# Attention stage of a hybrid DeltaNet/attention block: shared projection tiles spread over three turns each, evicted in the turn they end in, later gates loaded into the earlier gates' buffers, and the second projection's blocks moved into the last turn

## What is computed

```python
def merge(o_dn, o_na, gt, w_pa, w_pb, w_out):
    g_a, g_b = jnp.split(jax.nn.sigmoid(gt), 2, axis=-1)
    return (g_a * (o_dn @ w_pa) + g_b * (o_na @ w_pb)) @ w_out
...
    s_nb = jnp.where(col_mask[:, :, None, :], s_nb + bias.astype(jnp.float32), -jnp.inf)
    s_ctx = jnp.einsum('bpcqhd,bjhd->bhpcqj', qb, k_ctx, preferred_element_type=jnp.float32)
    m = jnp.maximum(jnp.max(s_nb, axis=(-2, -1)), jnp.max(s_ctx, axis=-1))
    e_nb = jnp.exp(s_nb - m[..., None, None])
    e_ctx = jnp.exp(s_ctx - m[..., None])
    denom = jnp.sum(e_nb, axis=(-2, -1)) + jnp.sum(e_ctx, axis=-1)
```

## Time and profile before

| | us |
|---|---|
| median of 3 runs | 1408.74 |
| lowest, highest | 1407.41, 1413.54 |
| profiled execution, its own time | 1407.62 |
| its span in the profile | 1405.8 |
| mean granted TensorE clock in it | 0.993 |

### The profile page before, as it was taken

The page is one execution under the profiler, slowest core; times in us unless marked ns, Lnnn a source line. Parts: engine busy times, 40 slices in busy tenths (PEclk is TensorE's granted clock), DMA queues, the critical chain, the costliest instruction groups (busy, mean ns, idle before and its releaser), DMA issues.

```text
span 1405.8 us, 26274 instructions
## 1 busy us (share of the span) xinstructions
PE 1358.4 (97%) x10442; PEld 1270.0 (90%) x10442; DVE 814.2 (58%) x1739; ACT 672.3 (48%) x1480; POOL 224.0 (16%) x189
## 2 busy tenths in 40 slices
PE   5999999999999999999999998999999999999998
PEld 4888989899998989999897877999999999999998
DVE  6466655756565565656535654757866434666422
ACT  4463736455373645537346554436655212555321
POOL 1020020202002020200030322000344002444100
PEclk8999999999999999999999999999999999999999
DMA  9552533142333324213426223522232322332332
GB/s 312 201 139 75 153 95 111 55 132 74 89 107 95 111 56 140 66 59 113 130 70 218 68 69 117 169 76 61 60 91 61 103 73 68 103 90 62 83 90 68
DMA packets 202560, 144.49 MB, mean 103 GB/s; under 512 B 8719, under 2 KB 188215, under 8 KB 202183
## 3 DMA queue, kind: packets, MB, share of 16 engines
q1 hardware_dynamic: 202439, 142.82, 34.3%
HBM read 126.77 MB, written 17.99 MB: 103 GB/s over the span
## 4 chain that ended last, share of the span: by engine, by line
PE 75%; DVE 12%; ACT 6%; issue 3%; SPq 2%; DMA 2%; POOL 0%; DVEq 0%; ACTq 0%
PE ps L1199 23%; PE ps L1728 16%; PE ps L1765 11%; PE ps L1498 7%; PE ps L1425 2%; PE ps L1369 1%; DVE tri L2613 1%; PE ps L1432 1%; PE ps L1273 1%; PE ps L1444 1%; DVE tri L2654 1%; DMA W<-in_w_in 1%; DVE W_r L2607 1%; PE ps L1443 1%; PE ps L1375 1%
## 5 line engine op out<-in xcount | busy, mean ns | idle before, releaser
L1199 PE MATMUL ps<-hT_r,WAH_r 128*128 128x320 f32 x912 | 228.4, 331 | 5.6 <-ACT zs L2061 2.4
L1199 PE MATMUL ps<-xT_r,WAH_r 128*128 128x320 f32 x912 | 207.4, 308 | 0.0
L1199 PEld LDWEIGHTS ps<-hT_r,WAH_r 128*128 128x128 f32 x912 | 145.0, 189 | 24.8 <-issue 11.5
L1199 PEld LDWEIGHTS ps<-xT_r,WAH_r 128*128 128x128 f32 x912 | 152.6, 188 | 0.0
L1199 PE MATMUL ps<-hT_r,W_r 128*128 128x320 f32 x592 | 133.9, 309 | 0.0
L1765 PE MATMUL ps<-a_part,W_r 128*128 128x320 f32 x704 | 132.3, 310 | 0.0
L3155 POOL TENSOR_TENSOR gm<-sqkq,dt 128x1280 f32<-128x1280 f32 x8 | 23.5, 2938 | 572.8 <-DVE Xc L2649 502.5
L1765 PEld LDWEIGHTS ps<-a_part,W_r 128*128 128x128 f32 x704 | 110.3, 188 | 0.0
L1728 PE MATMUL ps<-t_big_r,W_r 128*128 128x320 f32 x380 | 107.2, 310 | 0.6 <-ACT naT L2316 0.5
L1728 PE MATMUL ps<-b_part,W_r 128*128 128x320 f32 x456 | 101.4, 309 | 1.4 <-DVE oT_r L2925 1.4
L1199 PEld LDWEIGHTS ps<-hT_r,W_r 128*128 128x128 f32 x592 | 99.1, 189 | 0.0
(11 more groups left out here) (436 smaller groups left out, 3258.9 us busy)
## 6 DMA issues: line engine op xcount, KB each, us to landing
oT<-in_ffn_w SPq DMA_DIRECT2D x44, 512.0 KB, 5.2
W<-in_w_in SPq DMA_DIRECT2D x36, 512.0 KB, 4.0
WAH<-in_w_ada SPq DMA_DIRECT2D x18, 1024.0 KB, 6.8
naT<-in_w_in SPq DMA_DIRECT2D x24, 512.0 KB, 4.2
oT<-in_ffn_w SPq DMA_DIRECT2D x16, 704.0 KB, 4.6
ext_dram<-naT SPq DMA_DIRECT2D x28, 320.0 KB, 4.1
GCB<-gc_dram SPq DMA_DIRECT2D x7, 640.0 KB, 4.2
W<-in_w_pa SPq DMA_DIRECT2D x8, 512.0 KB, 3.7
```

The source lines that it names most:

```text
L1199: m = e.matmul(ps[:, bank + b, 0:n], w[:, k, :], x[:, k, a:a + n], start=k == 0 and i == 0, stop=k == KD - 1 and i == 2, skip_group_check= ...
```

## The change

- `pa_slots`: tile 1 has slots 0 to 7. Tile n from 2 on starts in turn 3n - 4 and has slots 1 and 2 of that turn, and slots 0, 1 and 2 of each of the two turns after it. From turn 2 on no block stands in the fourth slot of a turn, nor in the first slot of a tile's first turn. Tiles end in turns 1, 4, 7, 10, 13, 16 and 19.
- `PA_OUT`: a tile is evicted in VectorE's turn of the same number as TensorE's turn in which it ends, and `pa_evict` stands behind `for_next_pair` in it. `PA_HI` and `PA_LO` move to turns 3n - 6 and 3n - 5, so that `pa_lo_of(n + 1)` stands right behind `pa_evict(n)` in one turn for n from 1 to 6. `pa_evict(0)` moves ahead of three `o_small`.
- `tB` is gone: the later gates are loaded into `tA`. Those of tiles 0 and 1 are loaded when w_pa's tiles 6 and 7 have been evicted, and SP's chain of waits is gone. The loads of w_out's first two tiles now stand behind the eviction of tile 7 in SP's order.
- Blocks (1, 0), (1, 1), (1, 2) and (1, 3) of the second product are placed around block (0, 3), behind `PT` of the last unit instead of the last `out`.
- Waits for the stores of new_k and new_v move from SP to ScalarE and VectorE.

```diff
@@ -195,19 +195,22 @@
 
 def pa_slots():
 
-    return {(n - 1) * (2 * G) // (KD - 1) + k: (n, k) for n in range(1, KD) for k in range(KD)}
+    slots = {k: (1, k) for k in range(KD)}
+    for n in range(2, KD):
+        slots.update({4 * (3 * n - 4) + at: (n, k) for k, at in enumerate((1, 2, 4, 5, 6, 8, 9, 10))})
+    return slots
 
 
 PA_AT = pa_slots()
-PA_LAST = {0: -1, **{n: slot // 4 for slot, (n, k) in PA_AT.items() if k == KD - 1}}
-PA_OUT = {PA_LAST[n] + 1: n for n in range(1, KD)}
-PA_HI = {PA_LAST[n - 2] + 1: n for n in range(2, KD)}
-PA_LO = {PA_LAST[n - 2] + 2: n for n in range(2, KD)}
+PA_LAST = {n: slot // 4 for slot, (n, k) in PA_AT.items() if k == KD - 1}
+PA_OUT = {turn: n for n, turn in PA_LAST.items()}
+PA_HI = {3 * n - 6: n for n in range(2, KD)}
+PA_LO = {3 * n - 5: n for n in range(2, KD)}
 NA_HI = {NT * (p + 1) + 2: p for p in range(KP - 1)}
 NA_LO = {NT * (p + 1) + 4: p for p in range(KP - 1)}
 PB_HI = {PAIRS_OF_HEADS - 3: 0, PAIRS_OF_HEADS - 2: 1}
 PB_LO = {PAIRS_OF_HEADS - 2: 0, PAIRS_OF_HEADS - 1: 1}
-assert len(PA_AT) == KD * (KD - 1) and len(PA_OUT) == len(PA_HI) + 1 == KD - 1
+assert len(PA_AT) == KD * (KD - 1) and len(PA_OUT) == len(PA_HI) + 1 == KD - 1 and max(PA_AT) < 4 * PAIRS_OF_HEADS
 
 PE_FIRST = {1: "sums k", 2: "turn v", 3: "turn c", 4: "turn k"}
 PE_SECOND = {0: "sums q", 1: "sums c"}
@@ -690,7 +693,6 @@
         sb("under_pb", [P, 6 * TOK - 8 * KD], merging)
         pb_big = sb("pb_big", [P, 2, KP, P], merging, F32R)
         ysum = sb("ysum", [P, 2, TOK], merging)
-        tB = sb("tB", [P, 2, TOK], merging)
         yB = sb("yB", [P, 2, TOK], merging)
         merging.close()
 
@@ -965,7 +967,7 @@
                 e.dma_start(tA[:, n % 2, :], ext_dram[NA_N + n, :, :]).then_inc(ld_gate[n % 2], 16)
 
             def tB_in(n):
-                e.dma_start(tB[:, n % 2, :], ext_dram[NA_N + KD + n, :, :]).then_inc(ld_gate[n % 2], 16)
+                e.dma_start(tA[:, n % 2, :], ext_dram[NA_N + KD + n, :, :]).then_inc(ld_gate[n % 2], 16)
 
             def wo_in(n):
                 e.dma_start(wo_slot[n % 4], wo[:, :, n * P:(n + 1) * P]).then_inc(ld_o[n % 4], 16)
@@ -1042,14 +1044,11 @@
                 e.wait_ge(dve_na.sem, dve_na.after(f"k out {p}"))
                 e.dma_start(A["new_k"][0, 0].rearrange("t h d -> t (h d)")[:, p * P:(p + 1) * P], kout[:, :]).then_inc(st_k, 16)
 
-            tile_ended = {turn: n for n, turn in PA_LAST.items() if n and n + 2 < KD}
             for j in range(PAIRS_OF_HEADS):
                 p, i = j // NT, j % NT
-                if j in PA_OUT or not j:
-                    n = PA_OUT[j] if j else 0
-                    if n + 2 < KD:
-                        e.wait_ge(pa_out, n + 1)
-                        tA_in(n + 2)
+                if not j:
+                    e.wait_ge(pa_out, 1)
+                    tA_in(2)
                 if i == NT - 1 and p + 1 < KP:
                     for hh in range(2):
                         e.wait_ge(pool_na, 2 * CT * (p + 1) - 1 + hh)
@@ -1057,9 +1056,16 @@
                 if not i:
                     new_v(p)
                     new_k(p)
-                if j in tile_ended:
-                    e.wait_ge(pa_mm, tile_ended[j])
-                    pa_in(tile_ended[j] + 2)
+                if j in PA_OUT:
+                    n = PA_OUT[j]
+                    if n + 2 < KD:
+                        e.wait_ge(pa_mm, n)
+                        pa_in(n + 2)
+                    e.wait_ge(pa_out, n + 1)
+                    if n + 2 < KD:
+                        tA_in(n + 2)
+                    else:
+                        tB_in(n + 2 - KD)
                 if not i and 1 <= p < KP - 1:
                     e.wait_ge(pe_na.sem, pe_na.after(f"PV {j - 1}"))
                     cv_in(p + 1)
@@ -1068,15 +1074,6 @@
                 wo_in(n)
             e.wait_ge(st_x, 16)
             e.dma_start(xT[:, :, :], x_dram[:, :, :]).then_inc(ld_xT, 16)
-            e.wait_ge(st_k, 16 * KP)
-            e.wait_ge(st_v, 16 * KP)
-            e.wait_ge(st_S, 16 * 2 * H + 32)
-            e.wait_ge(act_na.sem, act_na.after(f"out {PAIRS_OF_HEADS - 1}"))
-            e.wait_ge(dve_na.sem, dve_na.after(f"P {G - 1}"))
-            e.wait_ge(pool_na, 2 * CT * KP)
-            e.wait_ge(pa_out, KD)
-            for n in range(2):
-                tB_in(n)
             for n in range(2, KD):
                 if n + 2 < KD:
                     e.wait_ge(pb_mm, n - 1)
@@ -1654,12 +1651,17 @@
             pb_block(0, 1)
             values(PAIRS_OF_HEADS - 1)
             pb_block(0, 2)
-            wait(act_na, f"out {PAIRS_OF_HEADS - 1}")
-            for n in range(KD):
+            wait(act_na, f"PT {G - 1}")
+            e.wait_ge(pb_lo, 2)
+            pb_block(1, 0)
+            pb_block(1, 1)
+            pb_block(0, KP - 1).then_inc(pb_mm, 1)
+            pb_block(1, 2)
+            pb_block(1, KP - 1).then_inc(pb_mm, 1)
+            for n in range(2, KD):
                 e.wait_ge(pb_lo, n + 1)
-                if n >= 2:
-                    e.wait_ge(y_sum, 2 * n - 3)
-                for k in range(0 if n else KP - 1, KP):
+                e.wait_ge(y_sum, 2 * n - 3)
+                for k in range(KP):
                     m = pb_block(n, k)
                 m.then_inc(pb_mm, 1)
 
@@ -2230,6 +2232,8 @@
             wait(dve_na, f"P {G - 1}")
             wait(pe_na, f"PV {PAIRS_OF_HEADS - 1}")
             e.wait_ge(pool_na, 2 * CT * KP)
+            e.wait_ge(st_k, 16 * KP)
+            e.wait_ge(st_v, 16 * KP)
             for n in range(KD):
                 if n + 2 < KD:
                     pb_hi_of(n + 2)
@@ -2811,12 +2815,11 @@
                 e.wait_ge(wo_hi, n + 1)
                 e.tensor_tensor(wo_small[n % 4], wo_slot[n % 4], wo_big[:, n % 4, :, :], ALU.subtract).then_inc(wo_lo, 1)
 
-            for k in range(KD - 1):
+            for k in range(KD):
                 o_small(k)
                 if k == KD - 4:
                     pa_lo_of(1)
-            pa_evict(0)
-            o_small(KD - 1)
+                    pa_evict(0)
             def minimum(g):
                 p, hh, c = UNITS[g]
                 _, _, (lo, hi) = key_tiles(c)
@@ -2874,9 +2877,9 @@
                     scaled_P(2 * j - 1)
                 else:
                     k_out(0)
+                for_next_pair(DVE_NEXT, j)
                 if j in PA_OUT:
                     pa_evict(PA_OUT[j])
-                for_next_pair(DVE_NEXT, j)
                 if j in PA_LO:
                     pa_lo_of(PA_LO[j])
                 if j in NA_LO:
@@ -2892,12 +2895,14 @@
             e.scalar_tensor_tensor(gain2[:, :, :], mods[:, 32:40, :], 1.0, cols[:, N2:N2 + 8].unsqueeze(2).to_broadcast([P, KD, 2]), ALU.add, ALU.mult).then_inc(mods_done, 1)
             e.tensor_scalar(mods[:, 16:24, :], mods[:, 16:24, :], 0.5, None, ALU.mult).then_inc(mods_done, 1)
             e.wait_ge(mods_done, 3)
+            e.wait_ge(st_v, 16 * KP)
+            e.wait_ge(st_k, 16 * KP)
             for n in range(KD):
                 i = n % 2
                 e.wait_ge(pb_mm, n + 1)
                 e.wait_ge(ld_gate[i], 16 * (KD // 2 + n // 2 + 1))
                 for b, (a, w) in enumerate(HALVES):
-                    m = e.scalar_tensor_tensor(yB[:, i, a:a + w], tB[:, i, a:a + w], 1.0, ps[:, 2 * i + b, 0:w], ALU.add, ALU.mult)
+                    m = e.scalar_tensor_tensor(yB[:, i, a:a + w], tA[:, i, a:a + w], 1.0, ps[:, 2 * i + b, 0:w], ALU.add, ALU.mult)
                 m.then_inc(y_sum, 1)
                 e.wait_ge(y_sum, 2 * n + 1)
                 if n >= 2:
```

## The result

| | before | changed |
|---|---|---|
| median, us | 1409.87 (4 runs) | 1417.26 (4 runs, 1416.61 to 1418.65) |
| profiled execution, us | 1407.62 | 1416.61 |
| its span, us | 1405.8 | 1414.8 |

What follows compares the result with a forecast made beforehand. TensorE, busy 97% of the span, was taken as the bound. Terms -8.0 + 0.5 + 16.0 - 1.95 gave +6.6 us, with +4.8 for the clock +11.4: median 1408.7 to 1420 us, range 1409 to 1425.

Steps and rivals of the forecast that it cites:

- waits that go in the turns: TensorE's waits for `PT`, `hT` and some scores in the turns vanish: 3.9, 3.0 and 1.1 us, 8.0 us saved.
- blocks apart: Pairs of blocks that lay side by side across a turn's border are separated: some 12 cases, 0.5 us lost.
- waits of the scores, turns 1, 4, 7, 10, 13, 16: Scores after tile ends wait for VectorE's eviction, split and two minima: six stalls of 2.1 to 3.2 us.
- another wait of scores, 853 us: In the turns, no second wait was seen behind the forecast stalls: 0 us.
- falls of the clock: Three of six new stalls bring TensorE's clock to half rate: 4.8 us lost; bounds none and 9.6 us.
- last turn, `P 38` and `P 39`: Turn 19: `P 38` stands behind eviction, `naT_r` and w_pb's small part on VectorE: 1.0 us lost.
- tail up to tile 2: Second product: blocks fill the `naT_r` wait, 1.0 us, and shorten tile 2's wait, 0.95 us: 1.95 us saved.
- tail, late loads: Third gate load queues behind xT and w_out on SP, so `yB` of tile 2 may wait: 0 taken, bounds 0 and 1 us.
- the earlier eviction of tile 0 brings nothing: Before scores(1): block (1, 0) starts some 1.4 us earlier, but scores(1) waits for the same VectorE work: 0 us.
- The first rival: In the turns, stalls come but the clock stays up: +6.6 us, 1415.3 us, from 1413 to 1418; chance 0.22.
- Half as long: In the turns, stalls are half as long and cancel the removed waits: -1.4 us, about 1407 us; chance 0.12.
- no stall: In the turns, `-max` is done early with eviction under TensorE's other work: -9.5 us, 1399 us; chance 0.06.

Runs made afterwards that it cites:

- split_first: Changed kernel with the split (small part of w_pa's next tile) ahead of the eviction in VectorE's turn; ratio 1.0014 to the kernel before.
- evict_next: Changed kernel with the eviction back in VectorE's next turn, behind both scaled_P and ahead of for_next_pair; ratio 1.0006 to the kernel before.
- between: Changed kernel with the eviction in VectorE's next turn, between the minima and scaled_P; ratio 0.9969 to the kernel before.
- fill_half: Changed kernel with two fillers (matmuls whose result nobody reads) behind the ends of tiles 1 to 6; ratio 1.0045 to the kernel before.
- between_xt3: between with the xT load cut into eight pieces, two at its old place, one behind each later gate load; ratio 0.9944 to the kernel before.
- xt_pieces3: Changed kernel with the xT load cut into eight pieces, two at its old place, one behind each later gate load; ratio 1.0080 to the kernel before.
- tail_xt: Kernel before with only the change's tail (later gates in tA, tile 1 around block (0, 3)) and xT's load in eight pieces; ratio 0.9984.

## Why the prediction was right, point by point

| step | forecast, us | measured, us |
|---|---|---|
| waits that go in the turns | -8.0 | -8.2 |
| blocks apart | +0.5 | about -0.3, what is left over |
| waits of the scores, turns 1, 4, 7, 10, 13, 16 | 3.2, 2.4, 2.2, 2.1, 2.4, 2.7 | 3.0, 2.3, 2.1, 2.0, 2.3, 2.6 |
| another wait of scores, 853 us | 0 | +0.2 |
| falls of the clock | +4.8 | +2.8 |
| last turn, `P 38` and `P 39` | +1.0 | +1.4 |
| tail up to tile 2 | -1.95 | -2.1 |
| tail, late loads | 0, bounds 0 and 1 | +1.0 |
| sum | +11.4 | +9.0 in the profiles, +7.4 by the medians |

*The stalls.* Each of the six was worked out from rows of before to within 0.2 us. split_first, evict_next and between show that the queue is the cause: the blocks stayed in their new places and the order on VectorE alone moved the turns from 127.9 to 120.9, 119.9 and 114.6 us. This part of the forecast was right by its mechanism.

*The waits that go.* All 13 waits in the turns after 752 us, 8.2 us in all, are gone. I had kept 0.3 us of them. That the earlier eviction of tile 0 brings nothing was right: block (1, 0) starts at 748.2 in place of 749.8, and scores(1) at 751.4 in both.

*The clock* is the term that was mis-sized. I took three falls at 1.6 us; the trace has two, and fill_half prices one at 1.4 us. Three of the six stalls was a choice between bounds, and no row of before could tell it from two or none; that it came near was luck in part. The Trainium skill (TensorE: Matmul & The Clock Gate, "A second HAM failure mode: psum-queue depth-cycling") says that short idles, repeated often enough, make the gate swing. The trace agrees in part: falls stand behind two of the six stalls. The first rival, stalls with the clock up, would have ended 2.8 us lower in the turns. That is all that the traces hold against it: it forecast +6.6 us, which is nearer to the +7.4 us of the medians than my +11.4 us is.

*The tail.* Up to tile 2 the forecast holds: block (0, 2) to tile 2 took 8.6 us and takes 6.4 us. Tile 2 itself waits 0.9 us where I had 0.8. In the last turn I counted the wait of `turn_P(38)` and not that `turn_P(39)` waits for its own scaling behind it. For the late gate load I took the lower bound, and the upper one came: from tile 2 to w_out it took 21.8 us and takes 22.8 us. ScalarE waits 0.9 us for w_pb and VectorE 0.9 us for the gate, waits for DMAs in the changed kernel:

```profile
DVE yB L2905 <- DMA tA<-ext_dram: 0.9, 1, 0.9
...
ACT pb_big L2140 <- DMA W<-in_w_pb: 0.9, 1, 0.9
```

*What cancelled.* The sum is closer than its terms. The clock was 2.0 us too high, blocks apart 0.8 us and the six stalls 0.7 us; the late loads were 1.0 us too low and the last turn 0.4 us.

*The rivals.* "Half as long" and "no stall" are out as forecasts of this kernel. The second named its own condition, `-max` ahead of the eviction. between fulfils it, and between_xt3, with the load of xT cut up besides, then reaches 8 us of the 9.5 us that it priced.

*Open.* The profiles are 9.0 us apart, the medians 7.4 us. The two agree within the interval, and single runs of the kernel before spread by 6 us, of the changed kernel by 2 us. Which stall brings the clock down is not settled, and the number of falls is that of single profiles: xt_pieces3 repeats both falls behind the same two stalls, but the first scores' wait near 752 us was followed by a fall in eleven of the twelve profiles and not in tail_xt.

## What to carry to other kernels

When work of a helper engine is moved, list what stands behind it in that engine's order up to the next thing that the busy engine waits for, add it up, and set it against what the busy engine still has to do. Here 3.3 to 3.6 us stood against 0.4 to 1.5 us, six times over. The eviction belongs behind the instruction that gates the next work (`-max`), not ahead of it, and work that only needs doing some time earlier (the split) belongs ahead of the wait. And when stalls are taken out, the transfers behind a big load in the same queue may be the next to be late: cut it up, and put the pieces behind the loads that are needed first.

## What the runs showed of the hardware that was not expected

- The length of a stall alone does not decide about the clock. In the changed kernel it fell behind waits of 2.96 and 2.34 us, and stayed behind waits of 2.60, 2.27, 2.11 and 1.99 us. split_first had a fall at 841 us, right behind its longest wait (2.27 us), where the changed kernel with the same wait had none.
- A fall needs no idle of TensorE ahead of it. In evict_next PE is busy for all of the 22 us up to 77 us, and the clock falls at 78.3 us (it did so near 77 us in three more of the twelve profiles, and not in the other eight, with the same work). Ahead of it, from 74.8 to 77.0 us, PE ran twenty matmuls of one column. These four profiles reach the turns about 1 to 2 us later:

```profile
55.00:77.00 22.00, 22.00 (x172) 20.99 (x170) 13.44 (x33) 15.10 (x36) 0.00 (x0) 1.00 0.27 74
78.30:81.70 3.40, 3.40 (x15) 3.40 (x14) 0.73 (x4) 1.43 (x3) 0.00 (x0) 0.51 0.90 256
```

- Runs of one kernel differ with their mean granted clock. Fourteen runs of the kernel before on one chip took from 1406.2 us at 0.995 to 1411.1 us at 0.989, 0.8 us for each 0.001.
- A plain float32 matmul of 512 columns appears as two passes, each starting 0.45 us behind the last, which is why four fillers took 3.6 us.
